# Value products of three differential pairs split into rounded parts by GpSimd, on one Trainium2 core

## The reference, cut to what matters

```python
def diff_block(qp, q):
    s = jnp.einsum('bqhmd,bkhmd->bhmqk', q.astype(f32), kd) * SCALE
    bias = table[t5_bucket(kpos[None, :] - qp[:, None])]
    s = s + jnp.transpose(bias, (2, 0, 1))[None, :, None]
    mask = (kpos[None, :] // CHUNK) <= (qp[:, None] // CHUNK)
    s = jnp.where(mask, s, NEG_INF)
    p = jax.nn.softmax(s, axis=-1)
    a = p[:, :, 0] - lam * p[:, :, 1]
    return jnp.einsum('bhqk,bkhe->bqhe', a, vd)
```

## Time and profile before

| | |
|---|---|
| median of 3 runs | 2802.86 us (2800.92 to 2806.03) |
| span of the profiled execution | 2803.1 us |
| PE busy | 2697.1 us (96%) |
| DVE busy | 1184.0 us (42%) |
| ACT busy | 1083.4 us (39%) |
| POOL busy | 255.9 us (9%) |
| PE's share of the chain that ended last | 86% |

### The profile page before, as it was taken

How to read it: one execution, slowest core, us unless ns; L and a number is a source line. 1 busy time by engine, 2 the same in 40 slices (tenths; PEclk the granted TensorE clock), 3 DMA queues, 4 the chain that set the end, 5 groups by cost and what they waited for, 6 DMA issues and landing times.

```text
span 2803.1 us, 37797 instructions
## 1 busy us (share of the span) xinstructions
PE 2697.1 (96%) x15257; PEld 2162.7 (77%) x15257; DVE 1184.0 (42%) x1847; ACT 1083.4 (39%) x2182; POOL 255.9 (9%) x270
## 2 busy tenths in 40 slices
PE   5999999999999999999989999999999999999998
PEld 4788888889999999999865665566566556888897
DVE  3421224315443332443333464365355446655554
ACT  3123331112122222100356676676666667422221
POOL 0100001131000000112230000000000003100000
PEclk9999999999999999999989999999999999999999
DMA  3453334448776766766651405053250503544442
GB/s 105 130 155 107 105 106 139 140 141 220 216 204 188 204 168 169 206 192 162 168 130 28 100 23 123 5 121 70 58 118 5 123 16 115 163 136 136 135 125 94
DMA packets 405774, 353.71 MB, mean 126 GB/s; under 512 B 45440, under 2 KB 368968, under 8 KB 399416
## 3 DMA queue, kind: packets, MB, share of 16 engines
q1 hardware_dynamic: 396464, 332.66, 44.1%
q0 software_dynamic: 9136, 18.63, 2.0%
HBM read 250.23 MB, written 100.71 MB: 125 GB/s over the span
## 4 chain that ended last, share of the span: by engine, by line
PE 86%; ACT 4%; DVE 3%; DMA 2%; issue 2%; POOL 1%; SPq 1%; DVEq 0%; ACTq 0%; POOLq 0%
PE p_acc L834 13%; PE p_acc L836 13%; PE p_acc L835 13%; PE a_sa L1887 5%; PE a_sa L1890 5%; PE a_sb L1907 4%; PE a_op L1936 4%; PE a_sb L1916 4%; PE a_op L1933 3%; PE p_turn L865 2%; PE e_U L1390 2%; PE e_U L1391 2%; PE e_U L1392 2%; ACT a_sa L1762 2%; ACT a_e L1791 2%
## 5 line engine op out<-in xcount | busy, mean ns | idle before, releaser
L834 PE MATMUL p_acc<-p_h_hi,p_w_hi 128*128 128x384 f32 (+1 forms) x1960 | 717.2, 366 | 9.8 <-DVE p_h_lo L652 5.8
L836 PE MATMUL p_acc<-p_h_hi,p_w_lo 128*128 128x384 f32 (+1 forms) x1960 | 702.0, 358 | 0.0
L835 PE MATMUL p_acc<-p_h_lo,p_w_hi 128*128 128x384 f32 (+1 forms) x1960 | 701.4, 358 | 0.0
L1813 DVE TENSOR_REDUCE a_nmax<-a_sa 128x1 f32<-128x1024 f32 (+7 forms) x384 | 349.4, 913 | 481.9 <-PE a_sa L1890 481.6
L1791 ACT ACTIVATE a_e<-a_sb 128x512 f32<-128x512 f32 (+3 forms) x640 | 317.9, 532 | 245.4 <-PE a_sb L1916 240.5
L834 PEld LDWEIGHTS p_acc<-p_h_hi,p_w_hi 128*128 128x128 f32 x1960 | 369.4, 188 | 45.2 <-issue 10.2
L836 PEld LDWEIGHTS p_acc<-p_h_hi,p_w_lo 128*128 128x128 f32 x1960 | 369.0, 188 | 31.5
L835 PEld LDWEIGHTS p_acc<-p_h_lo,p_w_hi 128*128 128x128 f32 x1960 | 369.8, 189 | 29.5
L1762 ACT ACTIVATE a_sa<-a_sa,a_nmax 128x1024 f32<-128x1024 f32 (+7 forms) x384 | 323.7, 843 | 73.3 <-DVE a_nmax L1813 71.9
L1887 PE MATMUL a_sa<-a_k,a_q 128*128 128x512 f32 (+4 forms) x640 | 261.6, 409 | 39.8 <-ACT a_sa L1762 33.3
L1907 PE MATMUL a_sb<-a_q,a_k 128*128 128x512 f32 (+2 forms) x640 | 272.5, 426 | 5.7 <-ACT a_e L1791 4.5
(11 more groups left out here) (217 smaller groups left out, 3490.4 us busy)
## 6 DMA issues: line engine op xcount, KB each, us to landing
p_raw<-in_w_in SPq DMA_DIRECT2D x98, 512.0 KB, 5.3
s_k_raw<-in_cache_fox_k SPq DMA_DIRECT2D x32, 512.0 KB, 6.9
s_v_raw<-in_cache_fox_v SPq DMA_DIRECT2D x32, 512.0 KB, 6.4
s_k_raw<-in_cache_diff_k SPq DMA_DIRECT2D x32, 512.0 KB, 7.1
s_v_raw<-in_cache_diff_v SPq DMA_DIRECT2D x32, 512.0 KB, 6.6
a_q<-scratch_q_hi SPq DMA_DIRECT2D x32, 512.0 KB, 13.8
a_k<-scratch_k_hi SPq DMA_DIRECT2D x32, 512.0 KB, 12.5
e_pair<-scratch_gT SPq DMA_DIRECT2D x80, 192.0 KB, 2.7
```

Of the source, the lines that this page charges most:

```text
L834: nc.tensor.matmul(acc[a % 2][:, 0:n], hi, h_hi[p][:, k, at:at + n], start=(k == 0), stop=False)
L835: nc.tensor.matmul(acc[a % 2][:, 0:n], hi, h_lo[p][:, k, at:at + n], start=False, stop=False)
L836: last = nc.tensor.matmul(acc[a % 2][:, 0:n], lo, h_hi[p][:, k, at:at + n], start=False, stop=(k == DK - 1))
L1813: nc.vector.tensor_reduce(nmax[:, b % 2, c, col:col + 1], scores_of(ev[1]), axes, ALU.max, negate=True).then_inc(a_maxed, 1)
```

## The change

For the differential pairs f = 1, 3 and 5 (not 7), V is done by three matmuls on rounded operands in place of one plain matmul: high values by high weights, high values by the remainder of the weights, and the remainder of the values by high weights. GpSimd makes the parts. For each unit it rounds the slot of `w` into `w_hi` (2 slots) by a `tensor_scalar` and subtracts it into `w_lo` (3 slots) by a `tensor_tensor`; in the first four units of a pair it does the same with a quarter of the values each (`VS`), into `v_hi` and `v_lo`. V waits for `w_lo_made` in place of `w_made`, and in the diagonal block also for `v_lo_made`. The rounding of a unit waits until V(u-2) is over.

```diff
@@ -1448,7 +1448,7 @@
     FT = 8
     pair_of = lambda f: f // 2 + 4 * (f % 2)
     ROW_C = HD + 2
-    E_SLOTS, W_SLOTS = 6, 3
+    E_SLOTS, W_SLOTS, HI_SLOTS = 6, 3, 2
     with ExitStack() as space:
         s.ctx = space
         maps = [[[s.sb(f"{n}_0{m}", [P, SEQ], F32R) for m in range(MAPS)] for n in ("q1", "k1", "q2", "k2")]]
@@ -1469,14 +1469,20 @@
             causal = s.sb("causal", [P, 2, P], BF16)
             v = [s.sb("v0", [P, PROMPT_TILES, P])]
             link["v0"] = v[0]
+            v_hi = s.sb("v_hi", [P, PROMPT_TILES, P], F32R)
+            w_hi = s.sb("w_hi", [P, HI_SLOTS, QUERIES], F32R)
         s.ctx = space
         s.sb("space", [P, 6 * D_MODEL])
         maps.append([[s.sb(f"{n}_1{m}", [P, SEQ], F32R) for m in range(MAPS)] for n in ("q1", "k1", "q2", "k2")])
         q1, k1, q2, k2 = ([maps[f][n] for f in range(2)] for n in range(4))
         e = s.sb("e", [P, E_SLOTS, MAPS, QUERIES])
-        w = s.sb("w", [P, W_SLOTS, QUERIES])
+        with ExitStack() as whole:
+            w = Scope(nc, whole, "a_", keep).sb("w", [P, W_SLOTS, QUERIES])
+        w_lo = s.sb("w_lo", [P, W_SLOTS, QUERIES], F32R)
         o = s.sb("o", [P, 2, QUERIES])
-        v.append(s.sb("v1", [P, PROMPT_TILES, P]))
+        with ExitStack() as whole:
+            v.append(Scope(nc, whole, "a_", keep).sb("v1", [P, PROMPT_TILES, P]))
+        v_lo = s.sb("v_lo", [P, PROMPT_TILES, P], F32R)
         band = s.sb("band", [P, 2, 3, BAND], BF16)
         sa = [s.ps(f"sa{i}", [P, CHUNK_KEYS]) for i in range(2)]
         cT = s.ps("cT", [P, 512])
@@ -1492,6 +1498,7 @@
     f_dve, f_act, c_turned = s.sem("f_dve"), s.sem("f_act"), s.sem("c_turned")
     c_in = [s.sem(f"c_in{i}") for i in range(2)]
     b_scored, e_made, w_made, multiplied = (s.sem(n) for n in ("b_scored", "e_made", "w_made", "multiplied"))
+    w_hi_made, w_lo_made, v_hi_made, v_lo_made = (s.sem(n) for n in ("w_hi_made", "w_lo_made", "v_hi_made", "v_lo_made"))
     o_made = s.sem("o_made")
     stored = [s.sem(f"stored{i}") for i in range(2)]
 
@@ -1510,6 +1517,7 @@
     NA, NU = len(A_UNITS), len(B_UNITS)
     NUF = NU // FT
     is_diff = lambda b: b // BLOCKS % 2 == 1
+    in_parts = lambda b: is_diff(b) and b // BLOCKS < FT - 1
     n_diff = list(itertools.accumulate([0] + [is_diff(b) for b, kt in B_UNITS]))
     a_width = lambda a: min(CHUNK_KEYS, (4 * (a[0] % BLOCKS) + a[2] + 1) * P - CHUNK_KEYS * a[3])
     a_first = {b: min(i for i, a in enumerate(A_UNITS) if a[0] == b) for b in range(NB)}
@@ -1605,6 +1613,8 @@
             out += [("B", u), ("E", u)]
             if u >= 1:
                 out.append(("W", u - 1))
+            if in_parts(b) and u - b_first[f * BLOCKS] < 4:
+                out.append(("VS", f, u - b_first[f * BLOCKS]))
             share = pass_a(target(u))
             if not finish:
                 next(share, None)
@@ -1730,6 +1740,26 @@
                     nc.gpsimd.memset(k2[1][m][HD:HD + 2, :].bitcast(F32), 0.0).then_inc(ones_set[1], 1)
             elif ev[0] == "MERGE":
                 link["merge"]["gpsimd"](pool, [ev[1]])
+            elif ev[0] == "VS":
+                f, part = ev[1:]
+                if part == 0:
+                    pool.wait_ge(v_in[1], 16 * (f // 2 + 1))
+                n = f // 2 * 4 + part + 1
+                ts = slice(4 * part, 4 * part + 4)
+                nc.gpsimd.tensor_scalar(v_hi[:, ts, :], v[1][:, ts, :], 1.0, 1.0, ALU.mult, ALU.mult).then_inc(v_hi_made, 1)
+                pool.wait_ge(v_hi_made, n)
+                nc.gpsimd.tensor_tensor(v_lo[:, ts, :], v[1][:, ts, :], v_hi[:, ts, :].bitcast(F32),
+                                        ALU.subtract).then_inc(v_lo_made, 1)
+            elif ev[0] == "W" and in_parts(B_UNITS[ev[1]][0]):
+                u = ev[1]
+                cols, n = valid(u), n_diff[u + 1]
+                pool.wait_ge(w_made, n)
+                pool.wait_ge(multiplied, u - HI_SLOTS + 1)
+                nc.gpsimd.tensor_scalar(w_hi[:, u % HI_SLOTS, cols], w[:, u % W_SLOTS, cols], 1.0, 1.0,
+                                        ALU.mult, ALU.mult).then_inc(w_hi_made, 1)
+                pool.wait_ge(w_hi_made, n)
+                nc.gpsimd.tensor_tensor(w_lo[:, u % W_SLOTS, cols], w[:, u % W_SLOTS, cols],
+                                        w_hi[:, u % HI_SLOTS, cols].bitcast(F32), ALU.subtract).then_inc(w_lo_made, 1)
             elif ev[0] == "F" and ev[2] == 4:
                 b = ev[1]
                 f, Q = b // BLOCKS, b % BLOCKS
@@ -1919,8 +1949,12 @@
         def product(u):
             b, kt = B_UNITS[u]
             z, Q = b // BLOCKS % 2, b % BLOCKS
-            if is_diff(b):
+            if is_diff(b) and not in_parts(b):
                 pe.wait_ge(w_made, n_diff[u + 1])
+            elif is_diff(b):
+                pe.wait_ge(w_lo_made, n_diff[u + 1])
+                if kt % 4 == 0 and b % BLOCKS == kt // 4:
+                    pe.wait_ge(v_lo_made, b // BLOCKS // 2 * 4 + kt // 4 + 1)
             else:
                 pe.wait_ge(e_made, 2 * u + 2)
             if kt == 0 and b % BLOCKS == 0:
@@ -1929,8 +1963,13 @@
                 pe.wait_ge(o_made, b)
             final = kt - 4 * Q == 3
             cols = valid(u)
-            if is_diff(b):
+            if is_diff(b) and not in_parts(b):
                 last = nc.tensor.matmul(op[:, cols], v[z][:, kt, :], w[:, u % W_SLOTS, cols], start=(kt == 0), stop=final)
+            elif is_diff(b):
+                hi, lo = w_hi[:, u % HI_SLOTS, cols], w_lo[:, u % W_SLOTS, cols]
+                nc.tensor.matmul(op[:, cols], v_hi[:, kt, :], hi, start=(kt == 0), stop=False)
+                nc.tensor.matmul(op[:, cols], v_hi[:, kt, :], lo, start=False, stop=False)
+                last = nc.tensor.matmul(op[:, cols], v_lo[:, kt, :], hi, start=False, stop=final)
             else:
                 for m in range(MAPS):
                     last = nc.tensor.matmul(op[m * HD:(m + 1) * HD, cols], v[z][:, kt, m * HD:(m + 1) * HD],
```

## The result

The changed kernel takes 2831.26 us (median of 4 runs, 2828.24 to 2839.15) against 2804.45 us (4 runs, 2800.92 to 2808.25). The ratio is 1.0096, with a 95% interval from 1.0078 to 1.0113: the change costs about 27 us, and was forecast to cost 19. In every run that has both figures the span is 1.7 to 1.8 us shorter than the time (2828.0 against 2829.84), so the profiled execution of the kernel before, with its span of 2803.1, stood about 2.0 us above the median of then, and not 0.2; the forecast of about 2822 does not move by it, since it is the median plus 18.9.

The account below looks back on a forecast made before the run. PE was taken to set the pace; per pair, stalls of 4.4 + 2.5 + 1.9 + 1.5 us less savings of 4.9 - 0.9 gave +6.3, three pairs +18.9 on 2803.1: about 2822 us, range 2793 to 2842.

Parts of the forecast that it names:

- the likeliest case: Stalls of PE in pairs 1, 3 and 5 about as reckoned: 2809 to 2830 us, likeliest near 2822, chance 0.55.
- more is lost: the clock: Rival: stalls of 2 to 3 us halve the clock at start and middle of each pair; 2830 to 2845 us, chance 0.12.
- What bounds the kernel: In a differential pair PE is busy 118.2 of 122 us at full clock and sets the pace.
- What PE saves: Three rounded matmuls cost 0.70 us against 0.86 for a full plain product: 4.9 us a pair, 14.6 for three.
- The split costs 2.1 us and shuts DVE out: From W's end to PE's release 2.1 us for 512 columns; DVE and POOL exclude each other during two-input instructions.
- The walk: Late splits unit by unit in a pair: start 4.4 us, units 13 to 15 2.5, 23 to 26 1.9, 29 to 32 1.5.
- The sum of a pair: Stalls 4.4 + 2.5 + 1.9 + 1.5 less savings of 4.9 - 0.9: +6.3 us a differential pair.
- signs of being wrong: V's weight-load waits under 5 us a pair, clock falls inside the pairs, or DVE's maxima rather than V holding PE.
- Two more signs: If right: POOL busy near 100 of a pair's 125 us, V's weight-load waits 8 to 13 us, longest at units 3 and 30.
- The rival that the splits stay hidden: GpSimd's splits do not delay PE and only savings count: 2788 us, or about 2795 with unit 3's stall; chance 0.2.

Follow-up runs that it names:

- the run with the splits alone: Changed kernel with GpSimd making the parts unused, PE multiplying plain weights and values and waiting for VectorE alone: 2809.19 us against 2805.63, ratio 1.0008.
- the run of the three matmuls alone: Changed kernel without GpSimd parts: three rounded matmuls of a map tile by weights VectorE writes rounded, output not attention: 2796.38 us against 2805.63, ratio 0.9959.

## Why the prediction was right, point by point

The direction, the cause and the range held. The time did not fall in the likeliest case (2809 to 2830, given 0.55) but 1.3 us above it, in the case "more is lost: the clock" (0.12).

- **What bounds the kernel.** PE, and its stream stops for whatever is late. Held; the run with the splits alone shows that POOL and DVE may be as busy as in the changed kernel at no cost that the measurement can tell from none.
- **What PE saves (4.9 us a pair, 4.0 of it had).** Direction right, 3.3 measured. The pace of the parts was right, that of 128 columns too (estimated 0.11 us; 2094.04 to 2094.43 for three, the first with its weight load behind the wait). Mis-sized is the part that is not had: I put it into the last 12 units, but some of it is lost in the middle of the pair as well, to waits for ACT as far as it was traced.
- **The split costs 2.1 us and shuts DVE out.** Held: 0.62 and 1.28 us, 0.08 to 0.09 between; W of 1.41 and 1.70 us. Wrong was the 0.24 us that I added for the weight load ahead of the matmul: after a wait both start together (2094.04), and the first matmul of 512 columns then takes 0.34 us to the next instead of 0.235 (2122.67 to 2123.01), so it costs 0.1.
- **The walk.** Against the run of the three matmuls alone, and counted from the product that opens one block to that which opens the next (the first from the pair's start, the last to its end), pair 5 lost 3.3 us in block 0 (predicted 4.4), nothing in block 1 (none), 3.1 in block 2 (3.5, units 13 to 15 and 23) and 3.9 in block 3 (2.4). The sum is 10.3, as predicted, but by luck: two errors cancel. The start was too long since POOL's small splits follow one another faster than reckoned (unit 0 was on time, unit 1 0.7 us late, not 1.3). The last block was halved on the argument that PE already waits for ACT there; but the stall at unit 30 stood in full (1.9 us of wait), and in the three units behind it another 0.9 us went, under half clock.
- **The sum of a pair.** +6.3 predicted, +7.1 measured in pair 5, where the clock falls only behind unit 30.
- **The clock, a rival with 0.12.** It came true in part, on top of the forecast, and with it one of the prediction's own signs of being wrong, a fall of the clock inside the pairs. I had it at nothing in the sum; the stall at the start was followed by half clock in pairs 1 and 3 and cost 2.6 and 1.5 us there (27.2 and 26.1 us against 24.6). Pairs 1, 3 and 5 are longer by 9.8, 8.6 and 7.1 us, together 25.5 where 18.9 was predicted: 4.1 of the difference is the clock at the start of pairs 1 and 3, the rest is the 0.8 us a pair above. The profiled spans differ by 24.9 us; in them pair 2 is 2.1 us longer as well, and the part ahead of the first block's copy 3.1 shorter (1460.7 against 1463.8). What is left to the 27 us between the medians is not placed.
- **Two more signs.** POOL was to be busy near 100 us of a pair and is 82; the prediction's own terms add up to about 83 (28 splits at 1.93 us, 13 for the smaller ones, 7.8 for values, 16 copies at 0.52). The waits of the weight loads were to be 8 to 13 us a pair and are 12.1, the longest at unit 3, as said.
- **The rival that the splits stay hidden** drew on pair 7, where DVE's delays cost nothing. The run with the splits alone repeats just that, and the argument against it (V now waits for POOL too) is what decided.

Not shown is the size of what shutting out adds at units 13 to 15 apart from the splits' own length; no run took one away and kept the other. Nor is it known why the clock falls behind one stall and not behind another of the same length, or for how long; no run set that by itself.

## What to carry to other kernels

A helper engine with two thirds of its time in use can still be late for each of its customers: read the distance from when the input is ready to when the result is due, unit by unit, and put what has no deadline (splits of values, DMA issues) elsewhere in its queue. A chain that grew by 2 us wants its consumer one unit later. Here this and the earlier split of the values were both needed before the cheaper arithmetic paid, and then by 0.3%, part of which the later place brings by itself. Moving work to another in-order queue needs the same question again: what is queued behind it.

## What the runs showed of the hardware that I had not expected

- The same stall of 2.32 us, in the same program at the same place, was followed by half clock for 6.8, 3.4 and 0 us, which cost 2.6, 1.5 and 0 us. So such a stall can cost twice its own length. One of 1.68 us was followed by 6.8 us in one pair and by none in another.
- Three rounded matmuls of 128 columns run at 0.11 us each, as fast as their weight loads follow one another, so narrow tiles lost nothing beyond that.
